# Stick-breaking attention in five steps per pair of heads instead of four, one unit of up to eight key blocks in each

## What is computed

```
def one_block(args):                       # branch B, 128 queries of every head
    z = einsum('bhtd,bshd->bhts', q_blk, k) * (D ** -0.5)
    causal = kpos[None, :] < qpos[:, None]
    log_keep = where(causal, -softplus(z), 0.0)
    between = cumsum(log_keep, axis=3, reverse=True) - log_keep
    w = where(causal, exp(log_sigmoid(z) + between), 0.0)
    return einsum('bhts,bshd->bhtd', w, v)

def hybrid_layer(x, ...):
    h = einsum('bsd,de->bse', x, w_in) + b_in        # q, k, v, gates of both branches
    y_a = (swa_sink_attention(rope(q_a), rope(k_a), v_a) * silu(gate_a)) @ w_up_a
    y_b = (stick_breaking_attention(q_b, k_b, v_b) * silu(gate_b)) @ w_up_b
    merged = sigmoid(mg_a) * y_a + sigmoid(mg_b) * y_b
    return layer_norm(alpha * x + merged @ w_out, ln_g, ln_b)
```

## Time and profile before

| | |
|---|---|
| median of 3 runs (lowest, highest) | 751.67 us (751.63, 752.24) |
| time of the profiled execution | 752.24 us |
| its span, first to last instruction | 750.5 us |
| PE busy in the span | 736.3 us, 98% |
| DVE, ACT, POOL busy | 516.8 us, 405.4 us, 109.1 us |
| branch B, from the first scores to the end of the last values | 179.87 to 457.92 us, 278.05 us |
| PE, DVE, ACT busy in it | 275.60, 218.78, 187.16 us |

### The profile page before, as it was taken

How to read it: one execution, slowest core, us unless ns; L and a number is a source line. 1 busy time by engine, 2 the same in 40 slices (tenths; PEclk the granted TensorE clock), 3 DMA queues, 4 the chain that set the end, 5 groups by cost and what they waited for, 6 DMA issues and landing times.

```text
span 750.5 us, 10645 instructions
## 1 busy us (share of the span) xinstructions
PE 736.3 (98%) x3940; PEld 577.2 (77%) x3940; DVE 516.8 (69%) x759; ACT 405.4 (54%) x760; POOL 109.1 (15%) x130
## 2 busy tenths in 40 slices
PE   8999999999999999999999999999999999999996
PEld 7888877776777777777777778888877888888884
DVE  6997888755897777869786974455584465570644
ACT  6954476665766756666666764555583122140321
POOL 0000000001322222223232210000000000000792
PEclk9999999999999999999999999999999999999998
DMA  8235322220101021020103123455536433350451
GB/s 308 86 98 125 115 72 87 69 85 28 57 15 43 18 69 56 2 86 0 57 1 99 57 71 127 141 194 192 191 133 230 169 126 127 113 217 8 139 188 67
DMA packets 41204, 76.22 MB, mean 102 GB/s; under 512 B 12224, under 2 KB 16320, under 8 KB 41152
## 3 DMA queue, kind: packets, MB, share of 16 engines
q1 hardware_dynamic: 41152, 75.54, 30.6%
HBM read 55.07 MB, written 18.35 MB: 98 GB/s over the span
## 4 chain that ended last, share of the span: by engine, by line
PE 88%; DVE 6%; ACT 3%; DMA 1%; issue 1%; POOL 0%; SPq 0%; ACTq 0%; DVEq 0%; POOLq 0%
PE ps L184 24%; PE ps L186 23%; PE ps L185 23%; PE ps L1520 5%; PE ps L1549 5%; PE ps L1536 4%; PE ps L1480 1%; PE ps L1453 1%; PE ps L1470 1%; DVE w_lo L1092 1%; DMA xr<-in_xt 1%; ACT beta_big L937 1%; DMA raw<-in_w 1%; DVE x_lo L1111 1%; DVE t_ops L1111 1%
## 5 line engine op out<-in xcount | busy, mean ns | idle before, releaser
L184 PE MATMUL ps<-x_hi,w_hi 128*128 128x512 f32 x416 | 168.7, 406 | 1.1 <-DVE x_lo L1149 0.7
L186 PE MATMUL ps<-x_hi,w_lo 128*128 128x512 f32 x416 | 162.6, 391 | 0.0
L185 PE MATMUL ps<-x_lo,w_hi 128*128 128x512 f32 x416 | 162.3, 390 | 0.0
L184 PE MATMUL ps<-t_ops,w_hi 128*128 128x512 f32 x304 | 122.9, 404 | 0.3 <-DVE w_lo L1092 0.3
L186 PE MATMUL ps<-t_ops,w_lo 128*128 128x512 f32 x304 | 118.9, 391 | 0.0
L185 PE MATMUL ps<-t_ops,w_hi 128*128 128x512 f32 x304 | 118.5, 390 | 0.0
L1092 DVE TENSOR_TENSOR w_lo<-raw,w_hi 128x512 fp32r<-128x512 f32 x120 | 81.9, 698 | 44.1 <-ACT w_hi L678 44.1
L184 PEld LDWEIGHTS ps<-x_hi,w_hi 128*128 128x128 f32 x416 | 78.1, 188 | 28.5 <-issue 10.7
L186 PEld LDWEIGHTS ps<-x_hi,w_lo 128*128 128x128 f32 x416 | 78.1, 188 | 17.0
L185 PEld LDWEIGHTS ps<-x_lo,w_hi 128*128 128x128 f32 x416 | 78.3, 188 | 14.3
L1231 DVE TENSOR_TENSOR_SCAN keep_big<-keep_big 128x1023 f32<-128x1023 f32 (+3 forms) x32 | 63.4, 1981 | 35.8 <-POOL keep_big L623 33.9
(11 more groups left out here) (182 smaller groups left out, 1211.1 us busy)
## 6 DMA issues: line engine op xcount, KB each, us to landing
raw<-in_w SPq DMA_DIRECT2D x28, 512.0 KB, 4.3
raw<-in_w SPq DMA_DIRECT2D x44, 256.0 KB, 2.9
sig_d<-sig_m SPq DMA_DIRECT2D x32, 256.0 KB, 3.5
sig_m<-sig_d SPq DMA_DIRECT2D x16, 512.0 KB, 4.2
xr<-in_xt SPq DMA_DIRECT2D x16, 256.0 KB, 6.8
raw<-in_xn SPq DMA_DIRECT2D x8, 512.0 KB, 3.6
out<-o_t SPq DMA_DIRECT2D x16, 256.0 KB, 2.2
o_t<-o_d SPq DMA_DIRECT2D x7, 512.0 KB, 4.9
```

Source lines behind the costliest of these rows:

```text
L184: pe.matmul(out, w_hi, x_hi, start=first, stop=False, skip_group_check=goes_on)
L185: pe.matmul(out, w_hi, x_lo, start=False, stop=False, skip_group_check=goes_on)
L186: return pe.matmul(out, w_lo, x_hi, start=False, stop=last, skip_group_check=goes_on)
```

## The change

A pair of heads has 5 steps in place of 4, and a step holds one unit of 8 key blocks, made of the query block with 8 - j key blocks and, for j = 1, 2, 3, the one with j key blocks behind it in the same tiles; the fifth step has the query block with 4 key blocks alone. There are 20 such units in place of 32. Scores, keep, beta, turning, copies and values are done for the unit as one; the selects and the scans are still one for each query block and head, the same number as before (64 keep selects, 32 beta selects, 64 scans). The pieces of the multiplication to weights are cut where a query block or a half of the tile ends, 12 in a pair as before. Keep has two buffers that alternate, beta has one.

On PE a step is now: values of the unit two steps before; scores; turn of group 0 of the unit before; a product; turn of groups 1 and 2; half a product; turn of group 3; half a product; and a product more, except in the fifth step. On ACT beta stands behind the copies of all groups of the unit before and waits for the last turn of that unit; `after` of the step's second product stands behind beta. On DVE the scans of head 0 and of head 1 are apart, with `after` of the first product between them, and `after` of the second product stands between the scans and the weights.

PE in the middle of a pair, before: the fourth step's start. `keep` and `v_n` mark values, `ks,qs` scores.

The diff, cut to its core:

```diff
-STEPS = 4 * PAIRS
+PER_PAIR = 5
+STEPS = PER_PAIR * PAIRS
...
+def parts(s):
+    j = s % PER_PAIR
+    if j in (0, PER_PAIR - 1):
+        return [(j, 0, 8 - j)]
+    return [(j, 0, 8 - j), (8 - j, 8 - j, j)]
...
-            keep_big = sb("keep_big", [P, 2, SEQ], F32, b)
-            beta_big = sb("beta_big", [P, 2, SEQ], F32, b)
-            keep_small = sb("keep_small", [P, 2, HALF], F32, b)
-            beta_small = sb("beta_small", [P, 2, HALF], F32, b)
+            keep0 = sb("keep0", [P, 2, SEQ], F32, b)
+            keep1 = sb("keep1", [P, 2, SEQ], F32, b)
+            beta = sb("beta", [P, 2, SEQ], F32, b)
...
# ACT
+            def betas(s):
+                w = P * key_blocks(s)
                 if s > 0:
+                    act.wait_ge(turned, ring_count(RING_AT["t", s - 1, step_banks(s - 1) - 1], False) + 1)
+                act.activation(beta[:, :, 0:w], z_both[:, :, 0:w], ACT.Sigmoid,
                                scale=SCALE).then_inc(beta_set, 1)
...
             for s in range(STEPS):
+                made_here = made(s)
+                keeps(s)
                 if s > 0:
+                    turned_blocks(s - 1, (0,))
+                read_bank(made_here[0])
+                if s > 0:
+                    turned_blocks(s - 1, (1, 2))
+                split_next(made_here[0])
+                if s > 0:
+                    turned_blocks(s - 1, (3,))
+                betas(s)
+                after(made_here[1])
+                if s % PER_PAIR == 0:
+                    turned_values(s // PER_PAIR)
+                    gate_b_sigmoid(s // PER_PAIR)
+                for q in made_here[2:]:
                     after(q)
...
# DVE
+                if 2 <= s < STEPS - 1:
+                    gated_out(s - 2)
+                break_sticks(s, 0)
+                after(made_here[0])
+                break_sticks(s, 1)
+                after(made_here[1])
+                weigh(s)
...
# PE
             for s in range(STEPS):
+                if s >= 2:
+                    values(s - 2)
+                scores(s)
                 if s > 0:
+                    turn(s - 1, (0,))
+                    product(made_here[0])
+                    turn(s - 1, (1, 2))
+                else:
+                    half_product(2 * STEP_0 + 1)
+                half_product(2 * made_here[1])
                 if s > 0:
+                    turn(s - 1, (3,))
+                half_product(2 * made_here[1] + 1)
+                if s % PER_PAIR == 0:
+                    turn_values(s // PER_PAIR)
+                for q in made_here[2:]:
+                    product(q)
```

More of the change, by code:

```diff
@@ L49 @@
 STEP_0 = 42
+STEP_END = STEP_0 + 2 * NP * PAIRS
 LAST_PAIR = NP * (N_PAIRS - 1)
@@ L103, in halves_done, with key_blocks, step_banks, tiles_before @@
     return 2 * h + n + 1
[L106 to L133, removed]
+def parts(s):
[3 more added lines that the diff above has]
+    return [(j, 0, 8 - j), (8 - j, 8 - j, j)]
+def key_blocks(s):
+    return 4 if s % PER_PAIR == PER_PAIR - 1 else 8
+def step_banks(s):
+    return key_blocks(s) // 2
+def tiles_before(s):
+    return sum(len(parts(i)) for i in range(s))
+def weight_pieces(s):
+    pieces = []
+    for h in range(key_blocks(s) // 4):
+        for _, at, n in parts(s):
+            first = max(P * at, HALF * h) + 1
+            end = min(P * (at + n), HALF * (h + 1) + 1)
+            if first < end:
+                pieces.append((h, first, end))
+    return pieces
+def pieces_before(s, half=0):
+    return sum(len(weight_pieces(i)) for i in range(s)) + sum(h < half for h, _, _ in weight_pieces(s))
+def turned_block(b):
+    return 2 * (0, 2, 1, 3)[b // 2] + b % 2
+def made(s):
+    at = STEP_0 + 2 * NP * (s // PER_PAIR) + 3 * (s % PER_PAIR)
+    return range(at, at + (2 if s % PER_PAIR == PER_PAIR - 1 else 3))
 ROTATIONS = {6: (0, 0), 7: (0, 1), 9: (0, 2), 10: (0, 3), 16: (1, 0), 18: (1, 3), 19: (1, 1), 20: (1, 2)}
@@ L152, in ring_order @@
     order = []
[L153 to L162, removed]
+    for s in range(STEPS + 2):
+        if s >= 2:
+            order += [("o", s - 2, 0)]
+        if 1 <= s <= STEPS:
+            order += [("t", s - 1, g) for g in range(step_banks(s - 1))]
+        if s < STEPS and s % PER_PAIR == 0:
+            order += [("v", s // PER_PAIR, g) for g in range(2)]
     return order
@@ L540, in _ @@
             for s in range(STEPS):
[L541 to L546, removed]
+                for q in made(s):
+                    after(q)
+                    if s % PER_PAIR == 1 and s > 1 and q == made(s)[0]:
+                        p = s // PER_PAIR - 1
+                        sp.wait_ge(o_set, SB * (p + 1))
                         sp.dma_start(o_d[4 + p], o_b[p % 2][:]).then_inc(ob_out, 16)
-            for q in range(STEP_0 + NP * STEPS // 2, N_PRODUCTS):
+            for q in range(STEP_END, N_PRODUCTS):
                 if q in (LAST_PAIR + 1, LAST_PAIR + 2):
@@ L1240, in gated_out, with weigh @@
-            def gated_out(s, small):
-                i = 2 * s + small
-                p, t = s // 4, unit(s, small)[0]
-                o = o_b[p % 2][:, P * t:P * (t + 1)]
-                dve.wait_ge(o_done, i + 1)
-                if s % 4 == 0:
+            def weigh(s):
+                dve.wait_ge(beta_cut, tiles_before(s + 1))
+                dve.wait_ge(scanned, 2 * tiles_before(s + 1))
+                for _, first, end in weight_pieces(s):
+                    dve.tensor_tensor(beta[:, :, first:end], beta[:, :, first:end],
+                                      keep[s % 2][:, :, first - 1:end - 1], ALU.mult).then_inc(w_ready, 1)
@@ L1505, in turn_values, with scores @@
                     last.then_inc(turned, 1)
-            def scores(s, small):
-                i, p = 2 * s + small, s // 4
-                tb, nb = unit(s, small)
-                if i > 0:
-                    pe.wait_ge(beta_set, i)
-                if s % 4 == 0 and not small:
+            def scores(s):
+                p = s // PER_PAIR
+                if s > 0:
+                    pe.wait_ge(beta_set, s)
+                if s % PER_PAIR == 0:
                     wait_block(pe, pair_kq(p), 0, 1)
```

264 lines of the change are left out of this document (104 added, 160 removed).

## The result

The changed kernel takes 739.66 us (median of 4 runs, 739.23 to 740.09), the kernel before 751.65 (median of 4, 751.10 to 752.24). The ratio is 0.984, with an interval of 0.9823 to 0.9857. So it is 12.0 us faster, where 9.4 were forecast: the direction is right, the time stands at the lower end of the range.

What follows compares the result with a forecast made beforehand. PE was taken to bound the kernel, by its paces and edges: 6.4 (edges) + 3.3 (old waits) - 0.3 (new wait) = 9.4 us less, 751.67 - 9.4 = 742.3 us. The final range was 739.5 to 746.5.

Steps and rivals of the forecast that it cites:

- What bounds the kernel: PE, busy 275.60 of 278.05 us in the changed stretch, read from start to start as paces plus extras where kinds meet.
- Edges, 6.4 us: On PE, 12 fewer places of values with scores, each with 0.53 us independent of key blocks: 6.4 us less.
- Seams in merged units: Scores of one query block following another's inside a merged unit: taken as 0 extra, upper end 2.4 us.
- Rival C: Each query block in a merged unit keeps its own drain in scores and values: gain 3.6 us less, 746; 4%.
- A transpose behind scores: Scores followed by a transpose, 19 times on PE: same extra as a product, no change; ends 3.8 less, 1.9 more.
- Rival D: A transpose drains nothing behind scores: 3.8 us less than the forecast, 738.5 us; 5%.
- The waits of before: PE waits at first turning (0.82), values behind their copy (0.9) and behind turned v (1.6): together 3.3 us, removed.
- The new wait at the first step: The weights' multiplication ends about when PE comes at the first step: 0.3 us left for it, bounds 0 and 0.8.
- The new order is not late: ACT and DVE chain delivers first weights before PE wants them: cover 1.4 us (7 and 1), 0.6 (fifth step), about 2 otherwise.
- The point at which the gain is eaten up: Delay of the weights from which the change would turn out slower: about 2.2 us.
- Rival A: Weights somewhat late, 8 to 12 steps losing 0.3 to 0.5 us, 2.5 to 6 us: 745 to 748.5; 13%.
- rival B: POOL selects and DVE scans hold each other up, weights late, 1.1 us in each of 12 steps: 755, slower; 5%.

## Why the prediction was right, and where it was short

**What bounds the kernel** was right: PE, by its pace and its edges, and the stretch lost 12.0 us with the same matmuls, products behind it the same.

**Edges, 6.4 us.** Right in mechanism and size. Start to start with three digits an edge place is 0.197 (scores) + 0.151 (values) + 0.096 and 0.105 (product matmuls ahead and behind) = 0.55 us, 12 of them 6.6. The runs with split scores and split values put a price of 0.43 and 0.39 us on the two halves by themselves.

**Seams in merged units, 0, and up to 2.4.** The value taken was right: with two query blocks scores take 1.93 us in place of 1.92 and values the same 1.90. Rival C falls.

**A transpose behind scores, taken as dear as a product.** This term was mis-sized. It costs 0.06 us and not 0.105: 19 x 0.045 = 0.85 us more gain, shown by the run that moves group 0. Rival D had it at nothing with scores' own end too, 3.8 us; that end stays, since scores take 35.0 us both with transposes behind them and with products (the same run). The Trainium skill ("TensorEngine Tiling (Array Packing)", section "Key Properties") says that changing the tiling mode drains TensorE. The trace agrees in that every such change in the rows has its extra, but the rule gives no size, and my inference from it, that a transpose pays what a product pays, was too high.

**The waits of before, 3.3 us.** Right: all three kinds are gone. They are 3.4 us with 0.1 at one group of eight transposes that takes 0.91 us in place of 0.79. The run with v turned late makes a wait for a copy of v again, at about 1 us a place.

**The new wait at the first step, 0.3.** It is 0.03 us by the scores' time from start to start, at the lower end of 0 to 0.8, and luck had a part in it: the weights come just in time, and with 1.2 us more in front of them that step lost the whole of it.

**No term at all** had the products' own pace. Of the 5.9 us that products lost, 1.7 are waits, 1.2 the matmul ahead of values and 2.3 (net of more matmuls behind transposes) those behind scores; 0.7 are left. Scores and turning now touch, so that the products stand in 61 runs and not 81, and a matmul deep in a run is faster than the second to fourth. The run that adds 19 interruptions gives about 0.025 us each, 0.5 for 20. I took 0.23 us for each matmul, which can't show this.

Together: 6.6 + 3.4 + 0.85 + 0.7 + 0.15 (the first scores no longer stand behind transposes of v) = 11.7 of the 12.0. The last 0.3 us are unassigned.

**The new order is not late.** Right, and the covers were near: 1.4 worked out and 1.0 measured in the tight two-block step, 0.6 and 0.64 in the fifth, 2 and 1.95, 1.9. That DVE is the next bound is shown by the added reductions. What the working missed is the second thread by which DVE holds PE, the output that frees a bank; in the changed kernel no wait for it shows, but a delay of 1.2 us brings it out. The point at which the gain is eaten up was put too late, at a delay of about 2.2 us: that counted the 12 two-block steps alone, and with 2.4 us more on DVE PE waited for the weights in 20 places.

**Rival A** (weights late by a few tenths in many steps) and **rival B** had chances of 13% and 5%. Neither is there. B's mechanism is, in the changed kernel itself too: two selects of head 1 take 1.96 us together, the first of them 1.59, because a scan of head 0 is running.

```profile
258.75 1.96 POOL L645 TENSOR_SCALAR_AFFINE_SELECT keep<-keep 128x128 f32<-128x128 f32 x2 [0.36 <-ACT keep L951]
```

But it stands in time that nobody waits for. One argument against B was too broad, that selects back to back take 0.29 us each: they do in 11 places where the scan came behind them, but 0.72 to 0.74 in 5 where DVE was at another operation with two inputs.

The range held the time, but by 0.2 us only: its low end was 739.5. Two small terms on the same side, the transpose behind scores and the pace of the products, each under 0.05 us a place, made 1.55 of the 2.6 us between the forecast and the gain, and a third one was the wait at the first step that didn't come.

## What to carry to other kernels

When the engine that bounds a kernel is busy throughout, measure its work from start to start by kind, and look for what is paid at each change of kind: here 0.55 us for every visit to values and scores, 18 us in 32 visits, which no idle column showed. Filling the unit (eight key blocks from two query blocks) takes visits away at no cost in work, as long as the other engines' chain keeps its cover (the time by which its result is there before it is wanted). Work the chain out for the shortest step as well as the fullest one, and count every thing that the late engine frees, not only the one that is wanted next.

## What the runs showed of the hardware

Four transposes take 0.41 us right behind float32 scores or values and 0.35 between products, 0.06 more; a product matmul right behind scores takes 0.105 us more than its pace.

Product matmuls take 0.231 to 0.233 us as the second to fourth of a run and 0.228 deep in it, and 19 interruptions more cost 0.5 us beside their own edges.

A GpSimd select that starts while a DVE scan runs ends with that scan or just behind it: in the changed kernel 27 of 39 end about 0.09 us after it and none later than 0.4, and a keep select so held takes up to 2.0 us where it takes 0.29 alone. A second select that stands ready behind the first goes ahead of the scan that the first one released: 0.29 to 0.30 us in 11 of the 12 two-block steps, though the scan started while it ran.
